# A two-layer hybrid trunk on eight cores: a cap on the Sync queue, scores per head, a second norm tile, output projections beside the gates, the last two tiles one after the other

## The reference

```
mod = silu(c) @ ada_w[l] + ada_b[l]        # 9 x 1024: shift, scale, gate, three times
y = rmsnorm(h) * (1 + sc1) + sh1
h = h + 0.5 * g1 * swiglu(y, wg1, wu1, wd1)
proj = (rmsnorm(h) * (1 + sc2) + sh2) @ w_in          # u, v (512 each), q, k, v (512 each)
out_a = gelu(u) * (tril(W_s) layernorm(gelu(v)) + b)  # 4 heads, chunks of 128 positions
out_b = mixture of three windowed attentions (window, stride): (128,1), (512,4), (2048,16)
                                                      # 8 heads of 64, rotary q and k
h = h + g2 * (concat(out_a, out_b) @ w_out)
h = h + 0.5 * g3 * swiglu(rmsnorm(h) * (1 + sc3) + sh3, wg2, wu2, wd2)
out = rmsnorm(h) * final_g                            # after both layers
```

## Time and profile before

| | |
|---|---|
| time, median of 3 runs | 5270.79 us (lowest 5268.8) |
| profiled execution | 5291.26 us |
| its span on the slowest core (core 5) | 5289.6 us; the other cores 5232.8 to 5271.2 us |
| PE / DVE / ACT / POOL busy on core 5 | 4882.8 / 2440.8 / 1906.1 / 1117.4 us |
| mean granted TensorE clock, core 5 | 0.965 |
| bytes moved by DMA | 910.29 MB, mean 172 GB/s |

### The profile page before, as it was taken

How to read it: one execution, slowest core, us unless ns; L and a number is a source line. 1 busy time by engine, 2 the same in 40 slices (tenths; PEclk the granted TensorE clock), 3 DMA queues, 4 the chain that set the end, 5 groups by cost and what they waited for, 6 DMA issues and landing times.

```text
span 5289.6 us, 73750 instructions; the slowest of 8 cores (5232.8 to 5289.6 us)
## 1 busy us (share of the span) xinstructions
PE 4882.8 (92%) x25298; PEld 2355.9 (45%) x25298; DVE 2440.8 (46%) x3978; ACT 1906.1 (36%) x2744; POOL 1117.4 (21%) x853
## 2 busy tenths in 40 slices
PE   4997779999879999998999998899998999999997
PEld 1443334555334555443444443455543455544443
DVE  4661353454445555364633335454534554534342
ACT  4110352444434545112122226354534454423221
POOL 2001271111461111201010116311146111021101
PEclk9999888999999999999999999999999999999998
DMA  7768644565746555888554864445474545385643
GB/s 197 199 176 220 177 115 123 142 180 158 196 134 208 167 174 147 247 232 256 181 179 129 229 183 129 126 135 171 138 210 134 201 128 174 103 265 189 194 134 102
DMA packets 368190, 910.29 MB, mean 172 GB/s; under 512 B 103600, under 2 KB 137776, under 8 KB 362928
## 3 DMA queue, kind: packets, MB, share of 16 engines
q1 hardware_dynamic: 270816, 657.56, 39.2%
q10 hardware_dynamic: 81216, 163.72, 9.7%
q0 software_dynamic: 15792, 84.29, 9.6%
HBM read 798.34 MB, written 243.27 MB: 197 GB/s over the span
## 4 chain that ended last, share of the span: by engine, by line
PE 75%; DMA 11%; POOL 4%; issue 3%; ACT 3%; DVE 2%; SPq 2%; ACTq 0%; POOLq 0%; DVEq 0%
PE ps L616 75%; DMA hS<-arena 5%; POOL arena L606 4%; ACT arena L603 2%; DMA arena<-xP 2%; DVE arena L609 1%; DMA arena<-mS 1%; SPq L1102 1%; DMA arena<-hS 1%; DMA qS<-arena 1%; DVE arena L606 1%; SPq L741 1%; DMA arena<-ada_w 0%; DMA arena<-wguS 0%; ACT L603 0%
## 5 line engine op out<-in xcount | busy, mean ns | idle before, releaser
L616 PE MATMUL ps<-arena 128*128 128x512 bf16 (+2 forms) x25298 | 4882.8, 356 | 390.8 <-POOL arena L606 115.9
L616 PEld LDWEIGHTS ps<-arena 128*128 128x128 bf16 x25298 | 2355.9, 101 | 2917.1 <-issue 603.2
L603 ACT ACTIVATE arena<-ps 128x512 f32<-128x512 f32 (+3 forms) x1408 | 932.2, 686 | 1972.4 <-PE ps L616 1867.2
L606 POOL TENSOR_TENSOR arena<-arena 128x1024 bf16<-128x1024 bf16 (+5 forms) x632 | 999.4, 1622 | 2376.2 <-ACT arena L603 2190.0
L603 ACT ACTIVATE arena<-arena 128x512 bf16<-128x512 f32 (+5 forms) x1122 | 758.3, 716 | 1088.0 <-DVE arena L609 443.2
L606 DVE TENSOR_TENSOR arena<-ps,arena 128x512 bf16<-128x512 f32 (+1 forms) x1216 | 818.2, 688 | 375.0 <-PE ps L616 261.7
L609 DVE SCALAR_TENSOR_TENSOR arena<-arena,ps 128x512 f32<-128x512 f32 x704 | 482.7, 687 | 955.5 <-ACT arena L603 954.5
L609 DVE SCALAR_TENSOR_TENSOR arena<-ps,arena 128x512 f32<-128x512 f32 (+1 forms) x456 | 336.1, 742 | 1053.7 <-PE ps L616 753.3
L609 DVE SCALAR_TENSOR_TENSOR arena<-arena 128x512 f32<-128x512 f32 (+2 forms) x398 | 352.2, 932 | 124.2 <-ACT arena L603 94.6
L606 DVE TENSOR_TENSOR arena<-arena 128x1024 bf16<-128x1024 bf16 (+3 forms) x398 | 261.1, 656 | 210.1 <-ACT arena L603 206.7
L603 ACT ACT_TABLE_LOAD x158 | 202.7, 1283 | 197.6 <-PE ps L616 133.1
(11 more groups left out here) (13 smaller groups left out, 27.5 us busy)
## 6 DMA issues: line engine op xcount, KB each, us to landing
arena<-wguS SPq DMA_DIRECT2D x308, 512.0 KB, 7.4
arena<-hS SPq DMA_DIRECT2D x216, 512.0 KB, 8.1
arena<-wdS SPq DMA_DIRECT2D x120, 704.0 KB, 8.4
arena<-ada_w SPq DMA_DIRECT2D x144, 512.0 KB, 7.5
hS<-arena ACTq DMA_DIRECT2D x240, 256.0 KB, 5.5
arena<-hS ACTq DMA_DIRECT2D x192, 256.0 KB, 3.0
wguS<-wgu POOLq DMA_DIRECT2D x66, 512.0 KB, 6.4
hS<-arena ACTq DMA_DIRECT2D x64, 512.0 KB, 9.9
```

Source lines behind the costliest of these rows:

```text
L603: return P.op("act", lambda e: e.activation(out=out, in_=in_, func=func, **kw), ns, reads, writes, accw, off=off, tset=tset)
L606: return P.op(eng, lambda e: e.tensor_tensor(out=out, in0=a, in1=b, op=op), ns, reads, writes, accw, off=off, name=name)
L616: x = e.matmul(o, lhsT=l, rhs=r, start=s0, stop=s1)
```

## The change

**Scheduler.** The bytes that SP has issued and that have not landed are held to WINDOW: a load or store on SP waits until earlier ones have landed, in the plan and, by added dependences, in the real program. Many planned durations are set nearer to those of the trace. **Start.** 16 buffers for the 16 columns, `fin` in pairs of channel chunks, tiles 0 and 1 both loaded ahead and summed by PE alone (4 x 2 matmuls of 512 columns). **Layer 0, stage a.** The downs' weights are converted in HBM during the gates (`conv` with kinds "d") and loaded as bfloat16; the casts of `w_in` are spread out; 24 of its `ada_w` columns move to stage c. **Norms.** Two tiles, `hbuf` and `hb2`, in turn; beside projections the squares are added on DVE, and PE sums two halves (2 matmuls instead of 1). **Projection.** The gating product goes from POOL to DVE, the rotary ring has 8 buffers instead of 4. **Output projection.** Two tiles of four stay in `o` and in `p`, the other two become side streams beside the gates of e and g; their buffers move. Tiles 6 and 7 are normed where they lie instead of being loaded again. **Attention.** Scores and Exp go head by head (each 512 columns on its own bank) instead of both at once; its spans are shorter. **End.** The last downs do all of tile 6 and then all of tile 7, with the eight weight tiles held, and tile 6's final norm beside tile 7's downs. The layout of `w_in` in SBUF and the first slot of the gates' ring change with it.

```diff
+    WINDOW = 2.6e6
@@ schedule
+            if e == "sp" and spb > self.WINDOW:
+                return None
...
+        k, b = 0, 0.0
+        for x in spq:
+            while b > self.WINDOW:
+                b -= T_[spq[k]].dma
+                T_[x].deps.add(spq[k])
+                k += 1
+            b += T_[x].dma
@@ norm_sum(h, how="pool", ss=None)
+                if how == "pe":
+                    mms([(bank(NB), mean_bf, ap[:, x, :], k + x == 0, k + x == KC - 1) for x in range(2)], 2 * MM, [b, bConst],
+                        [psB[NB]] if k == 0 else (), [psB[NB]] if k else ())
...
+            tt(how, a0, a0, a1, ALU.add, 2150.0 if how == "pool" else 740.0, reads=[b1], writes=[b0])
+            if how == "pool":
+                tt("pool", a0[:, 0, :], a0[:, 0, :], a0[:, 1, :], ALU.add, 1180.0, writes=[b0])
@@ MX.inner
-            self.tr = z.ring(4, [128, T], F32, 1, "tr")
+            self.tr = z.ring(8, [128, T], F32, 1, "tr")
@@ load_win
-                    reads=[mx.win[1][c]], writes=[bWI[l, c]], off=60000.0)
+                    reads=[mx.wb(c * 4)], writes=[bWI[l, c]], off=0.0, pace=P.M + wait)
@@ proj_tile, gating
-            tt("pool", oa[:, hd, :], zt, mx.ug[hd][0], ALU.mult, 1400.0, reads=[bzt, mx.ug[hd][1]],
+            tt("dve", oa[:, hd, :], zt, mx.ug[hd][0], ALU.mult, 925.0, reads=[bzt, mx.ug[hd][1]],
@@ attention, for h in range(2)
-                        mms(lst, ncol * 0.4213 + 5.0 * len(lst), [bq, bk], [psB[QB], psB[QB + 1]])
-                        act(pout, pin, AF.Exp, act_ns(2 * nel), TS_EXP, reads=[psB[QB], psB[QB + 1]], writes=[bp], off=200.0, scale=0.125)
+                            mms(lst, nel * 0.4213 + 6.0 * len(lst), [bq, bk], [psB[QB + h]])
+                            act(cust(pT, h * 512 + c0, fr), cust(bank(QB + h), c0, fr), AF.Exp, act_ns(nel), TS_EXP,
+                                reads=[psB[QB + h]], writes=() if h else [bp], accw=[bp] if h else (), off=200.0, scale=0.125)
@@ layer 0, start and stage a
-            hload(None, hbuf, 0, xP, bX, lead=80000.0)
+            hload(None, hbuf, 0, xP, bX, lead=82000.0)
+            hload(None, hx[0], 1, xP, bX, lead=81000.0)
+            conv(0, 0, "cv00", *span((L + "a.g0", 60000.0), (L + "a.g1", -40000.0)), kinds="d")
+            f.mode = "bf"
-            load_win(l, mx, "cast", -60000.0)
+            load_win(l, mx, "cast", (-90000.0, -60000.0, 5000.0, 25000.0, 45000.0), 90000.0)
+            hb2 = htile(mx.hlo)
-                    norm(l, 1, t, hS, bHS, y2[t])
+                    norm(l, 1, t, hS, bHS, y2[t], h=(hbuf, hb2)[t % 2])
@@ before gates c and e
+        ngu[0] += (2 - ngu[0]) % NGU
...
+        ngu[0] += (0 - ngu[0]) % NGU
@@ stages o, e
-        for t in range(4):
-            h = ht[t % 3]
-            outproj(l, t, wo, mxr[t % 2], h, PRB)
+        ht = [hbuf, hb2]
+        mxr = [(view(gu_lo + 8192 * k_, [128, KC, T], BF16), reg(gu_lo + 8192 * k_, gu_lo + 8192 * k_ + 8192, "mx")) for k_ in (1, 2)]
+        for t in (0, 1):
+            h = ht[t]
+            outproj(l, t, wo, mxr[t], h, PRB)
...
+        with P.side(L + "oq", *span((L + "e.g0", -4000.0), (L + "e.g0", 60000.0))):
+            for t in (2, 3):
+                outproj(l, t, wo, mxr[t % 2], ht[t % 2], (5, 6, 7))
-        attention(1, L + "at1", *span((L + "e.g0", 5000.0), (L + "f.g1", -5000.0)))
+        attention(1, L + "at1", *span((L + "e.g0", 70000.0), (L + "f.g1", -18000.0)))
@@ stages g, h
+        with P.side(L + "op", *span((L + "g.g0", -6000.0), (L + "g.g1", -40000.0))):
+            for t in (6, 7):
+                outproj(l, t, wo, mxr[t % 2], ht[t % 2], (5, 6, 7))
-            with P.side("ada1", *span((L + "g.g0", 10000.0), (L + "h.g1", -20000.0))) as S_:
+            with P.side("ada1", *span((L + "g.d0", -5000.0), (L + "h.g1", 0.0))) as S_:
-                norm(l, 2, t, hS, bHS, yv[t % 2])
+                norm_sum(ht[t % 2])
+                norm_mod(ht[t % 2], l, 2, yv[t % 2])
@@ end of layer 1
+            for m in range(KC):
+                f.down(0, m, wds[m], kt[0])
+            for m in range(KC):
+                f.down(1, m, wds[m], kt[1])
+            with P.side("fin6", *span("z1", ("z2", -8000.0))):
+                norm_sum(kt[0])
+                norm_fin(kt[0], 6)
+            with P.side("fin7", *span("z1", "z2")):
+                norm_sum(kt[1], "pe")
+                norm_fin(kt[1], 7, eng=("dve", "pool", "dve"))
```

335 lines of the change are left out of this document (189 added, 146 removed).

## The result

The changed kernel takes **0.9739** of the kernel before (95% interval 0.9682 to 0.9795), 2.6% less. On 5271 us that is 137 us, about 5133; the forecast was 5080 with a range of 4995 to 5210. In some executions of any of these kernels the cores of one die, at times of both, run at a granted clock of 0.81 to 0.96 and take up to 6058 us; such dies are left out of the comparisons of times here.

The account below looks back on a forecast made before the run. Matmuls bound most of the kernel, so gains come only where PE stands, nine windows of 374.7 us. Terms sum to -195 us against the 5271 median: 5076, given as 5080 us, range 4995 to 5210.

Parts of the forecast that it names:

- The end: Kernel's end: one of two norms moves beside the last downs, the other loses its POOL sums; -19 us (-10 to -24).
- stages p to g of layer 0: Layer 0: one norm wait of 15.90 us goes, its tile being normed where it lies; -12 us (+10 to -20).
- Layer 0's downs of a: Layer 0's stage a: fewer cast bytes shorten the residual slots' round trip, most of 44.1 us idle goes; -32 us (-10 to -44).
- Clock and added matmuls: Whole kernel: less of the lower clock level, -15 us (0 to -40); 54 more matmuls for the sums, +12.
- Layer 0's first projection: Norm and gate-weight waits go (-26.7 us), POOL's relief -14, `w_in` writes queueing +8; sum -33 (0 to -50).
- The start: Kernel's start: bytes ahead set the first gate, at about 55 us; 14 us sooner plus 6 after; -20 us (0 to -40).
- Layer 1's first projection: Layer 1: late gate weight of 13.68 us goes (-12), POOL's relief -8; sum -20 us (-5 to -30).
- The line "Added": Added work: 54 matmuls +12 us, attention head by head 0 (0 to +20), output projections beside gates +10 (0 to +40).
- stages n and o: Both layers: of 45.0 us of `mS` waits 2.5 remain, the other 48.5 shrink by 18; -60 us (-25 to -80).
- The waits move: Rival: an uncovered wait replaces each removed one, half of the 195 us comes back; about 5180 us, chance 0.17.
- the starving gates: Rival, four attention stretches: the cap on SP's bytes holds back the gates' weights; 5550 us, chance 0.07.
- The lower clock of dense stretches: Rival: stretches made dense from 411 to 1300 us get clock 0.81, losing 137 us; about 5215 us, chance 0.06.

Follow-up runs that it names:

- e10: Changed kernel without the early conversion of layer 0's first down weights, cast in the downs again: mean 5120 us, 10 more than the changed kernel.
- e7: Changed kernel with gating products and the norms' partial sums beside the projections back on POOL: mean 5115 us against 5110.
- e9: Changed kernel with every norm of input to the projections through one tile again: mean span 5174 us, overstated by slow-clock stretches on four cores; the other four 5147.
- e12: Kernel before with only a second tile for every second norm of input to the projections: 0.9992 by the slowest core, mean 5255 to 5243 us.
- e8: Changed kernel with the gates' first weights released behind the 4th ada_w column, not the 11th: first gate at 46 us, first downs at 386.0 us as before the edit.
- e5: Changed kernel with scores of both heads in one piece and all output projections in PE's main order: mean 5074 us, 0.966 of the kernel before.
- e3: Changed kernel with all output projections in PE's main order and the second attention from the start of e's gates: 0.9713 of the kernel before, mean 5091 us.
- e6: Changed kernel with the loads of h for norms beside the downs of d issued 33 us earlier, ahead of the winS loads: mean 5092 us, 18 less.

## Why the prediction was right, and where it was not

*Right as to mechanism and size.* The end: -18.3 us (forecast -19), and stages p to g of layer 0: -13.6 (-12); both are read from the traces, no run undoes either alone. The buffers of `mS`: 36 us alone (42.5 in my sum), and no `mS` wait is left. The limit on SP: 0. Of the signs that I named, the first gate came before 60 us (58.41), and PE's idle time came out at 267.6 us on core 7 (near 220 was to be seen, 406.8 before): the gain is short by what the next points take.

*Right in size, in part by luck.* Layer 0's downs of a with the stretch behind: -28.0 (-32); e10 shows 16 of it to be the early conversion. But I put all 44.1 us of idle time there down to the residual slots. PE's waits in that window of the earlier trace rows before the change, and in the same downs with it, are:

```profile
PE ps L616 <- DVE arena L609: 23.1, 4, 8.9
PE ps L616 <- POOL arena L606: 20.3, 3, 12.7
```

```profile
PE ps L641 <- POOL arena L631: 21.2, 4, 9.3
```

The waits on the slots, which DVE adds into, are gone; those on the sums of norms stay, all in the second downs. So some 21 us of idle time went, not most of 44. The rest of the gain is PE's busy time, 7 us less at the higher clock (0.88 in the earlier trace rows's window, 0.94 with the change), which I had counted in a term of its own. Nor is the cause the one that I worked out. The bytes did not fall: 184.6 us x 219 GB/s = 40 MB before, 41.7 MB with the change at a DMA share of 0.82. And in the second downs a slot still takes 19.9 us for its write and load, where I wanted under 15:

```profile
530.35 11.55 DMA hS<-arena
...
542.25 8.31 DMA arena<-xP
```

Why the slots no longer hold PE up with as many bytes is open.

*Clock and added matmuls*, -15 + 12: PE's busy time rose by 9 us in the sum of medians (4848 to 4857), so the clock gave back about 3 of the 15.

*Right in size, wrong in cause.* Layer 0's first projection: -39.7 (-33). I gave 14 us of it to POOL's relief, 18 to that in the two second projections and 8 in layer 1's first. e7 puts that work back in the changed kernel and nothing changes; the relief alone on the kernel before was not run. POOL was named in the earlier trace rows as the last link of a chain, and the POOL waits that are left stand in downs, where e7 changes nothing. What holds the gain is the second norm tile: it is worth 34.8 us of this stretch in the changed kernel (e9) and 39.1 alone (e12). I left out its price: with it the second downs ahead are 16.0 us longer (105.7 against e9's 89.7), so 18.8 us are left.

*Too large.* The start: -6.8 (-20). I bounded the first gate by bytes, and it came as I said; but the later gates also wait for the columns' reductions on DVE, which run from 26 to 57 us with hardly a pause (e8). Layer 1's first projection: -5.4 with the downs ahead of it (-20). The late weight is gone, but the norms of two tiles now crowd into the downs: +18.5 there, -23.9 behind.

*The step that failed.* The line "Added", and with it stages n and o. From the downs of d to those of g, both layers, the forecast was -60 and -6 and +10, so -56; it was -26.9. The removed waits were sized well: with scores and projections undone (e5) the same stretches are 56 us shorter than before, against 66. The two parts that I priced at 0 and +10 cost 14 and 20 us over the kernel, 29 of it here. For the scores I wrote that ACT's spare time covers them; the cover failed by 14 us. That average share is no cover for a unit that PE waits for one by one fits this, but no run shows it. (The Trainium skill, "ScalarE: Activation LUTs", section "What ACT_TABLE_LOAD costs", gives an ACTIVATE with immediate operands 186 ns and 0.833 ns an element: 612 and 1039 ns here. The rows, 595 and 1020, agree within 3%; an estimate by it puts the longer Exp list at 52 us of ACT, and 47 were measured.) For the projections I counted 64 evictions on DVE, and not that the second attention, whose buffers and banks they use, would start 65 us later and be packed tighter (e3, which undoes both at once). A third cost was not in my sum at all: 17 of 20 `winS` loads moved into the downs of d, among the loads of h for the norms there; e6 wins 20 us in the two stretches.

*The rivals.* "The waits move" is the one that took part of the gain. One place that it named, ACT in the norms beside the downs, is where e6 gained, though ACT as the reason is not shown there. Of the starving gates there is no trace: no `wguS` wait on core 7, at most 4.8 us on any core. The lower clock of dense stretches did not come: 0.979 over the span of core 7 with PE busy 95%. The Trainium skill's rule weighed there ("TensorE: Matmul & The Clock Gate", Part 1, the peak-current limiter) would have all eight cores at 13/16; in the profiled execution two cores were there, for about 160 us, and the trace decides.

## What to carry to other kernels

A wait's releaser is the last link of a chain: before moving work off the engine that is named, ask what that engine was waiting for, and put the work back once to see whether it mattered. When a step is moved beside other work, follow what it pushes: whose buffers it holds, whose loads stand behind its loads, which stage then starts later. A second buffer lets work run ahead, and part of its waits goes with it: count both places (39.1 us less in one stretch of e12, 23.4 more in those ahead). Price a finer hand-over by the fixed part of a call (595 ns for half of a 1020 ns call, so 170 ns more for each of 280 calls, 47 us) and not by the engine's average share. This gives what the engine has to do more; PE lost 14 us by it here.
